# Running the final RMSNorm inside the last down-projection, one 512-token block at a time

## The reference

```python
    h = rms_norm(x, norm2_g) * (1 + scale2) + shift2
    u = causal_depthwise_conv(h @ w_up, conv_w, conv_b)
    a, g = jnp.split(u, 2, axis=-1)
    y = (jax.nn.silu(g) * a) @ w_down
    return x + gate2 * y
...
    return rms_norm(x, final_g)      # x * rsqrt(mean(x*x) + 1e-6) * g, per token
```

## Time and profile before

| | |
|---|---|
| median of 2 runs | 2495.39 us (2495.37 to 2495.41) |
| the profiled execution, its own time | 2501.72 us |
| its span, first to last instruction, core 4 | 2500.6 us |
| spans of the 8 cores | 2472.0 to 2500.6 us |
| mean granted TensorE clock of the cores | 0.846 to 0.854 |
| busy: TensorE (PE) | 1930.2 us, 77% |
| busy: VectorE (DVE) | 1435.6 us, 57% |
| busy: ScalarE (ACT) | 1150.7 us, 46% |

### The profile page before, as it was taken

One profiled execution on the slowest core, in us unless ns is written; L12 is line 12 of the kernel. 1 busy time (PEld: TensorE's weight loads), 2 busy tenths in 40 slices (PEclk: granted clock), 3 DMA queues, 4 the chain that ended last, 5 costly groups with the idle time before them and its releaser, 6 DMA issues.

```text
span 2500.6 us, 34090 instructions; the slowest of 8 cores (2472.0 to 2500.6 us)
## 1 busy us (share of the span) xinstructions
PE 1930.2 (77%) x10680; PEld 998.0 (40%) x10680; DVE 1435.6 (57%) x2333; ACT 1150.7 (46%) x2198; POOL 312.3 (12%) x629
## 2 busy tenths in 40 slices
PE   1477877878753999999967787877763799999982
PEld 1454444444421444443423444444431344443431
DVE  0034454444445868787964454444435687878874
ACT  0024344443446837563814434443426774736535
POOL 2010000000010515221220000000001121212200
PEclk9997777878766999999987787878776899999995
DMA  8852011110050949641461000000003133332304
GB/s 224 155 77 22 9 18 18 18 14 1 3 56 5 101 43 112 59 47 18 47 101 19 1 1 1 1 1 1 1 1 42 20 33 43 34 39 26 47 1 135
DMA packets 215888, 99.51 MB, mean 40 GB/s; under 512 B 177696, under 2 KB 202656, under 8 KB 214688
## 3 DMA queue, kind: packets, MB, share of 16 engines
q0 software_dynamic: 188880, 70.91, 25.8%
q1 hardware_dynamic: 22096, 18.04, 2.5%
q10 hardware_dynamic: 4736, 8.39, 1.0%
HBM read 159.82 MB, written 8.39 MB: 67 GB/s over the span
## 4 chain that ended last, share of the span: by engine, by line
PE 50%; DVE 20%; ACT 13%; issue 10%; DMA 6%; DVEq 1%; ACTq 0%; POOL 0%; SPq 0%; POOLq 0%
PE ps L106 48%; DVE arena L127 10%; ACT arena L115 9%; DVE arena L118 8%; DMA arena<-ada_w 5%; PE ps L109 2%; ACT arena L131 2%; ACT L115 2%; DVE arena L696 1%; DMA arena<-gla_ba 1%; DVEq L211 1%; ACTq L211 0%; POOL arena L217 0%; SPq L217 0%; ACTq L217 0%
## 5 line engine op out<-in xcount | busy, mean ns | idle before, releaser
L106 PE MATMUL ps<-arena 128*128 128x512 bf16 (+10 forms) x9976 | 1876.6, 343 | 361.3 <-ACT arena L115 198.0
L106 PEld LDWEIGHTS ps<-arena 128*128 128x128 bf16 (+4 forms) x9976 | 955.0, 115 | 1262.6 <-issue 679.2
L118 DVE TENSOR_TENSOR arena<-arena 128x512 bf16<-128x512 f32 (+7 forms) x505 | 384.9, 772 | 283.5 <-ACT arena L115 262.3
L127 DVE SCALAR_TENSOR_TENSOR arena<-arena 128x512 f32<-128x512 f32 (+1 forms) x712 | 514.5, 744 | 38.2 <-DVE arena L127 1.4
L115 ACT ACTIVATE arena<-ps,arena 128x512 f32<-128x512 f32 (+4 forms) x520 | 338.1, 650 | 202.8 <-PE ps L106 99.6
L131 ACT COPY arena<-ps 128x512 f32<-128x512 f32 (+1 forms) x416 | 267.3, 642 | 267.4 <-PE ps L106 252.0
L115 ACT ACTIVATE arena<-arena 128x512 f32<-128x512 f32 (+8 forms) x644 | 321.4, 527 | 119.6 <-DVE arena L127 50.2
L118 DVE TENSOR_TENSOR arena<-ps,arena 128x384 f32<-128x384 f32 (+6 forms) x356 | 192.7, 549 | 319.8 <-PE ps L106 183.3
L127 DVE SCALAR_TENSOR_TENSOR arena<-ps,arena 128x512 f32<-128x512 f32 x320 | 239.7, 751 | 216.7 <-PE ps L106 216.7
L115 ACT ACT_TABLE_LOAD x74 | 94.9, 1283 | 331.5 <-PE ps L106 291.7
L109 PE MATMUL ps<-arena 128*48 128x128 bf16 (+1 forms) x704 | 69.5, 239 | 198.6 <-DVE arena L118 198.6
(11 more groups left out here) (15 smaller groups left out, 78.4 us busy)
## 6 DMA issues: line engine op xcount, KB each, us to landing
arena<-w_up POOLq DMA_DIRECT2D x88, 256.0 KB, 5.4
arena<-ada_w POOLq DMA_DIRECT2D x80, 256.0 KB, 6.4
arena<-w_down POOLq DMA_DIRECT2D x44, 256.0 KB, 7.5
arena<-w_in POOLq DMA_DIRECT2D x32, 322.0 KB, 15.8
arena<-ada_w SPq DMA_DIRECT2D x16, 512.0 KB, 4.3
arena<-xT ACTq DMA_DIRECT2D x4, 1024.0 KB, 17.7
arena<-xT SPq DMA_DIRECT2D x4, 1024.0 KB, 26.3
arena<-w_out POOLq DMA_DIRECT2D x16, 256.0 KB, 26.6
```

Source lines behind the costliest of these rows:

```text
L106: self.op('pe', lambda e: e.matmul(out, lhsT, rhs, start=start, stop=stop), r=[lhsT, rhs], w=[out])
L118: self.op(eng, lambda e: e.tensor_tensor(out, in0, in1, op), r=[in0, in1], w=[out])
L127: self.op(eng, lambda e: e.scalar_tensor_tensor(out, in0, scalar, in1, op0, op1), r=[in0, scalar, in1], w=[out])
```

## The change

`final` becomes a class `Final` that holds the same buffers, and its method `block(tb)` norms and sends out one block of 512 tokens. In the last layer and the last of the four groups, `ffn` calls `fin.block(tb)` right after the 8 output chunks of block `tb` are written down, so each block's norm stands in the program ahead of the next block's down-projection. The width of a step goes from 256 to 128 tokens (four steps per block, 16 in all), and each of the 16 output DMAs carries 512 KB in runs of 512 bytes where 8 carried 1024 KB in runs of 1024 bytes. Inside a block `norm_a` is one step ahead of `norm_b`; at a block's end it isn't. The scratch lies in the first 22.5 KB of the region that holds the FFN's `h2`, which the last up-projection has finished reading by then.

```diff
-    def ffn(l, nextmod=None):
+    def ffn(l, nextmod=None, fin=None):
...
                     P.stt(xs, pst[:, :], modT[:, l, 40 + m:41 + m], xs, ALU.mult, ALU.add)
+                if fin is not None and q + 1 == len(QUARTERS):
+                    fin.block(tb)
...
+    class Final:
+        def __init__(self):
+            RB = Bump(RB0, RB0 + KC * T * 2)
+            self.NT = 128
...
+        def block(self, tb):
+            NT = self.NT
+            n = 512 // NT
+            first = tb * n
+            norm_a(first * NT, NT, self.tmps[first % 2], psn=ps[6 + first % 2][:, 0:NT])
+            for i in range(first, first + n):
+                t0 = i * NT
+                if i + 1 < first + n:
+                    norm_a(t0 + NT, NT, self.tmps[(i + 1) % 2], psn=ps[6 + (i + 1) % 2][:, 0:NT])
+                norm_b(t0, NT, self.ob[:, i % 2], self.tmps[i % 2], G=col("gf"))
+                P.dma('sp' if i % 2 == 0 else 'act', ov[:, :, t0:t0 + NT], self.ob[:, i % 2], sem="out%d" % (i % 2))
...
-        NT = 256
...
-        nb = T // NT
-        norm_a(0, NT, tmps[0], psn=ps[6][:, 0:NT])
-        for i in range(nb):
...
-            ffn(l, nextmod=nxt)
-    final()
+            lastl = (li + 1 == len(layers))
+            ffn(l, nextmod=nxt, fin=(Final() if lastl else None))
```

More of the change, by code:

```diff
@@ L893, in ffn @@
             mod_finish(nextmod, 0, 48)
-    def final():
-        RB = Bump(RB0, RLIM)
-        NT = 256
[L898 to L905, removed]
-        nb = T // NT
-        norm_a(0, NT, tmps[0], psn=ps[6][:, 0:NT])
-        for i in range(nb):
[L909 to L913, removed]
+    class Final:
+        def __init__(self):
+            RB = Bump(RB0, RB0 + KC * T * 2)
+            self.NT = 128
+            self.tmps = []
+            for i in range(2):
+                sq = RB.alloc(KC * self.NT * 2, BF16, "p (k t) -> p k t", k=KC)
+                rstd = RB.alloc(self.NT * 4, F32)
+                lnv = RB.alloc(self.NT * 4, F32)
+                tmpf = RB.alloc(KC * self.NT * 4, F32, "p (k t) -> p k t", k=KC)
+                self.tmps.append((sq, rstd, lnv, tmpf))
+            self.ob = RB.alloc(2 * KC * self.NT * 4, F32, "p (s k t) -> p s k t", s=2, k=KC)
+            self.i = 0
+        def block(self, tb):
[9 more added lines that the diff above has]
+                P.dma('sp' if i % 2 == 0 else 'act', ov[:, :, t0:t0 + NT], self.ob[:, i % 2], sem="out%d" % (i % 2))
+    def final():
+        f = Final()
+        for tb in range(4):
+            f.block(tb)
     layers = list(layers)
@@ L935, in build @@
         if do_ffn:
-            ffn(l, nextmod=nxt)
-    final()
+            lastl = (li + 1 == len(layers))
+            ffn(l, nextmod=nxt, fin=(Final() if lastl else None))
+    if not (do_ffn and len(layers) > 0):
+        final()
     st = P.emit()
```

## The result

| | before | changed |
|---|---|---|
| median | 2496.6 us (10 runs) | 2514.12 us (11 runs) |
| ratio, 95% interval | | 1.0076 [1.0054, 1.0097] |
| span of the profiled execution | 2500.6 us | 2509.9 us |
| start of block 0's last addition | 2415.33 | 2409.91 |
| from there to the end of the span | 85.3 us | 100.0 us |

The changed kernel is 17.5 us slower by the medians, 0.8%; a few runs of both lay far above the rest, with a lower granted clock on one die, and the ratio leaves them out. The forecast was 2513.6. The last line of the table is the sharper number, since everything in front of block 0's last addition is the same program in both, and two executions differ there by 5 us. I call that stretch **the stretch** in what follows: it grew by 14.7 us.

A forecast was written before the change was run, and what follows sets the result against it. Down-projection bound by TensorE, the norm behind it by latency. Gaps 45.4, clock 6.9, table load 1.3 and tail 22.9 make 76.5 us against 58.3; 2495.4 + 18.2 = 2513.6 us, range 2503 to 2531.

The forecast's parts named there:

- The gap before each next block: Between blocks, TensorE is free 15.15 us after the last addition's start, once the fourth sum ends; three gaps, 45.4 us.
- The clock: After each gap, 4.85 us of projection run at the low clock: 2.3 us for each of three blocks, 6.9 in all.
- The table load: Moves from the end to block 0's first Ln, where TensorE waits for it: 1.28 us.
- The tail: Behind the last block, from its last addition's start through norm and final store landing: 22.9 us.
- The estimate of 3.2 us for 512 KB: Landing time of a final output DMA by the skill's formula; the forecast took 3.7, the sum would be 0.5 lower.
- no further stall, but no room either: Next block's first addition, behind the norm's multiplies on VectorE, ends about when TensorE needs it; later norm ends pass on.
- The sum: From block 0's last addition to the end without projections: 76.5 us against 58.3 before, so 18.2 us added.
- most of it is granularity: Final norm: 16 steps of about 4.5 us are 72 us, where 8 of 6.82 are 55.
- hidden after all: Rival: TensorE gets on with the next block during a norm; end 35.4 us earlier, giving 2460; 3%.
- The clock never comes back: Rival: clock stays at 0.50 through all 40 matmuls, each block paying 7.8 us; +34.7 in all, 2530; 7%.
- The stores are slow: Rival: a 512 KB output store takes 7 us, so the fourth step waits for its buffer; +11, 2525; 7%.

The follow-up runs named there:

- e3: The changed kernel plus filler matmuls into an unread PSUM bank ahead of each block's four sums, keeping TensorE busy; stretch 95.2 us, ratio 1.0041.
- e2: The changed kernel's block-by-block placement, with the 256-token steps of before in place of 128; stretch 89.0 us, ratio 1.0010.
- e8: The changed kernel with a block's four squares and four sums ahead of everything else of its norm; stretch 93.5 us, ratio 1.0030.
- e6: e2 with the multiplications of a block's second step moved behind the next block's first two additions; stretch 92.8 us, ratio 1.0033.
- e1: The changed kernel's 128-token steps, but all 16 at the end of the program as before the change; stretch 102.7 us, ratio 1.0069.
- e4: The changed kernel's instructions reordered: one 128-token norm step behind every second output chunk of the next block; stretch 63.8 us, ratio 0.9916.

## Why the prediction was right

The sign, the mechanism and the size hold: 2514.12 against 2513.6. Step by step, with the stretch as the measure:

- *The gap before each next block*: 15.15 forecast, 14.59, 14.57 and 14.54 measured without the table load (from the last addition to the end of the fourth sum; ahead of block 2, 2436.84 to 2451.41). Counted from the square, the sums came at 1.2, 3.76, 7.9 and 12.7 where 1.18, 3.75, 8.25 and 13.28 were forecast. Two terms were off, one each way: the final norm's Identities have no bias and write float32, and a step's Exp, four Identities and square take 2.43, not the 2.79 of rows 5; and the issue of a DMA on ScalarE cost 0.67 ahead of block 2 (4.81 against 4.14 between sums; 0.69 and 0.95 ahead of the other two), not 0.53.
- *The clock*: low for 5.1 us from the fourth sum in blocks 1 and 3, then 1.00, where 5.85 had been forecast. A block took 2.0 to 2.1 us more than its gap and 8.98, forecast 2.3. Block 2 tells what this is worth: there the clock rose after 3.3 us (0.64 is the mean of 2453 to 2454, 1.00 follows), 1.8 earlier, and the block was only 0.1 us shorter, because TensorE ran into VectorE's queue, the one wait of 0.7 us. So the 2.3 was about right as a number, but it wasn't the clock's alone: had the clock been high, VectorE's multiplications would have held the block nearly as long. e3 shows the same: with the clock held up, a block gives back only 1.1 to 1.3.
- *The table load*: 1.28, in the first gap, as forecast.
- *The tail*: 22.9 forecast, 21.9 measured, again the shorter Identities; the last store was over 3.6 us after its issue, forecast 3.7. The estimate of 3.2 us for 512 KB, worked out from the formula of the Trainium skill, "DMA: Bandwidth & Descriptors", section Anatomy of one DMA — SWDGE (gpsimd) path, is near the median landing of 3.3. The page fits that formula to DMAs issued by GpSimd; these are issued by SP and ScalarE.
- *VectorE "no further stall, but no room either"*: one wait of 0.7 us in three blocks. That sentence was the most important one, and I had used it only for the stall that wasn't there: in e2, e3 and e8 it was this second lock that took back what the first gave, and e6, which moved part of it, made it longer.
- *The sum*: 18.2 forecast, 14.7 in the stretch. The 3.5 are the gaps (43.7 in place of 45.4), the clock (6.2 in place of 6.9) and the tail (21.9 in place of 22.9), all three forecast too long. By the medians it is 17.5, with an interval of the ratio that spans 13.5 to 24.2 us and holds both. That the median fell within 0.6 us of the forecast is partly luck.
- *Where it goes*: "most of it is granularity" is shown by e1 (17.4 us lost with no placement at all, about 1.3 of it at the ends of blocks) and e2 (11.0 won back by width alone).

Of the rivals, *hidden after all* was excluded by the order on TensorE and became true when that order and VectorE's were changed together (e4: the stretch fell by 21.5, where the rival's full hiding would have given 35.4; the difference is VectorE's 14.3 us a block against TensorE's 9). *The clock never comes back*: it came back after 3.3 to 5.1 us. *The stores are slow*: 3.3 us in the median, 4.9 at most, no wait.

What stays open: every ratio of the table agrees with its stretch within its interval, but the intervals are 5 to 19 us wide, so the totals alone couldn't have told most of the variants apart. The stretch hardly varies, so the width comes from the common part, where executions differ by several us and the cores of one execution by up to 29; no run here says why.

## What to carry to other kernels

Placing code between two blocks didn't by itself overlap it with them: each engine here waits at the first instruction whose input isn't ready (34.7 us on TensorE), and the placement alone gave 2.7 us back with narrow steps and cost 3.7 with wide ones. Look on every engine separately for what the next block's first instructions stand behind. Count the locks before removing one: here the sums on TensorE and the multiplications on VectorE ended within 4 us of each other, and only weaving both, in pieces short enough for two PSUM banks to bridge (2.1 us), turned a stretch 14.7 us longer than before into one 21.5 shorter. Cutting the latency-bound chain into twice as many steps cost more here (17.4) than its early start gained.

## What the runs showed of the hardware

- Filler matmuls into an unread bank kept the granted clock at 1.00 through waits of 2 to 4 us (the mean of that time was 0.72 without them), and the 8 sums at 0.61 us in place of 1.01; they gained 4.8 us where the cold spells had been priced at 7 to 11.
- The time at the low clock after a wait isn't the same each time: after the same fourth sum the granted clock rose after 5.1 us in blocks 1 and 3 of the changed kernel and after 3.3 in block 2.
- A 1024 KB store in 1024-byte runs landed in 4.5 us, a 512 KB store in 512-byte runs in 3.3: half the bytes save a quarter of the time.
- An Exp and four Identities of 128x128 took 1.48 us in the final norm, with a scale alone and float32 out, and 1.85 in the FFN's norm, with scale and bias and bf16 out. Which of the two differences does it wasn't tried.
